# Two joined transformer blocks on one core: the norm between the blocks folded into the next stage, the second block's mixer reordered, start and tail changed

## The chip, the core and the metric

One core of a Trainium2 chip runs the whole program. Its engines are TensorE (PE, with its weight loads as PEld), VectorE (DVE), ScalarE (ACT), GpSimd (POOL) and SyncE (SP), which only issues transfers here. The metric is the time of one execution on the device in microseconds, the median of several runs. SBUF is the on-chip memory with 128 partitions, PSUM the eight banks into which TensorE writes.

## What is computed

Two different blocks follow each other on x with 256 tokens and 1024 channels in fp32. Each has two layers of FFN, mixer, FFN and ends in an RMS norm; the second block takes the normed output of the first.

```
for l in range(2):                                   # both blocks have this shape
    x = x + 0.5 * swiglu(rmsnorm(x, ffn1_norm[l]), ...)
    x = x + mixer(rmsnorm(x, mix_norm[l]))           # block 1: attention, gated recurrence, memory
    x = x + 0.5 * swiglu(rmsnorm(x, ffn2_norm[l]), ...)   # block 2: RWKV-7 group and retention group
x = rmsnorm(x, final_norm)
```

The second block's mixer projects to r, k, v and the low-rank parts, makes kk = k * k_k of unit length per head, runs the recurrence S <- S diag(w) + (S a) b^T + v k^T in chunks of 64 tokens, and beside it a retention group with rotary positions; both are gated and go through w_out.

## The kernel before

**Weights.** Every weight matrix comes in units of 1 MB (128 x 2048 fp32) through a ring of three slots in `raw`. `split_hi` (line 301, ScalarE) rounds a unit to `w_hi`, `split_lo` (line 306, VectorE) writes the remainder to `w_lo`, and TensorE multiplies high by high and low, and low by high (`mm3`, line 321; `mm`, line 326, also for all products that are not split). The next load into a slot waits for `lo_ready`, the next split for `unit_used`. Each engine has its own program in a fixed order; semaphores join them (`need` waits for a named step of another engine).

**Stages.** A stage number n counts FFNs and mixers. An FFN (`ffn_pe`, `ffn_act`, `ffn_dve`, from line 401) runs over 11 tiles: two hidden units and one output unit each. Its input is x times the norm's gain, split into `x_hi` (line 348, ScalarE) and `x_lo` (line 357, VectorE) by the stage in front of it, so that its first products need no statistics. `square_act` (line 352), `sq_sum_dve` (line 366) and `norm_pe` give the sum of squares in PSUM; `norm_dve` (lines 377 and 381) scales it and takes the reciprocal of the root that `norm_act` (line 373) takes, and the hidden values are multiplied by `rms` afterwards.

**Between the blocks** stands a stage of its own (`mid_stage`, function `between`): norm of x, x scaled by gain and rms on VectorE (line 2479), then x_hi, x_lo, squares and their sum for the next FFN. TensorE does only `norm_pe` there. The end has the same norm, with the gain on ScalarE (line 2445) and the product with `rms` on VectorE (line 2493).

**The second mixer** (`mix2_pe`, `mix2_act`, `mix2_dve`, from line 1729) has 18 units: LORA, K, UP, R, V, RQK, RV, RG and OUT2. The length of kk comes from four products with `sum_pairs` into 8 rows, a root, a reciprocal on VectorE (line 1941) and four products with `spread` back to 128 rows. The rotation of the retention's q and k (`rqk_rot`) stands after both RV units, and three VectorE steps follow (lines 1969 to 1971) before the scores `n` and `nt` may use their PSUM banks. Then come five levels (`LEVELS2`) that invert a triangular matrix by doubling: `w1` products, ScalarE's copy of w1 (line 1811), `z` and `zl` products, VectorE's predicated copies `take` (line 1895). Between them `first_fill` and `second_fill` put other products into banks 6 and 7, each of which VectorE or ScalarE must empty before the next. Both RG units run after the levels. A loop over the chunks (c from 1 to 3) passes the state between TensorE and VectorE (`new_u` line 2021, `new_state` lines 2029 and 2030); `y_centred` and the output units follow.

**SBUF.** Temporary tiles lie in an arena of 4 KB slots from `base`; `at(name, slot, ...)` places them by hand. `keep_warm(k, bank)` (line 1373) issues k products of a zero tile.

## Time and profile before

| | us |
|---|---|
| median of 3 runs | 2482.17 |
| the runs | 2477.22 to 2484.57 |
| profiled execution | 2484.07 |
| its span, first to last instruction | 2482.3 |
| TensorE busy in it | 2423.2 |
| VectorE, ScalarE, GpSimd busy | 1796.7, 1204.1, 111.6 |
| mean granted TensorE clock | 0.988 |

### The profile page before, as it was taken

The numbers are of one execution on the slowest core, as the hardware profiler recorded it, in microseconds if no ns is written. First come the engines' busy times: TensorE is split into PE (matmuls) and PEld (weight loads), VectorE is DVE, ScalarE is ACT, GpSimd is POOL, SyncE is SP. The second block draws the span as 40 slices with busy tenths as digits, with TensorE's granted clock in tenths as the row PEclk, the third lists the DMA queues.
The fourth block names the chain that finished last, engine by engine and source line by source line (L and its number), as shares of the span: only waits on it lengthen the run. The fifth ranks groups of instructions, "written<-read, shape, count | busy, mean of one in ns | idle before, by whom it ended". The sixth has DMA issues, their size and how long they took to land.

```text
span 2482.3 us, 46884 instructions
## 1 busy us (share of the span) xinstructions
PE 2423.2 (98%) x20196; PEld 2246.5 (91%) x20196; DVE 1796.7 (72%) x1608; ACT 1204.1 (49%) x1210; POOL 111.6 (4%) x71
## 2 busy tenths in 40 slices
PE   7999999999999999999998999999999999999998
PEld 6999999999899999999997999898998999988997
DVE  7877777777787767868777777756767767756766
ACT  5445656544544456555444445634445445635443
POOL 0000251000000004400000000000000000000000
PEclk9999999999999999999998999999999999999999
DMA  8555444565555555445554555413555655503652
GB/s 272 194 187 180 138 147 127 170 203 186 170 191 195 172 164 156 136 153 171 194 191 132 193 186 164 151 37 113 193 187 168 202 186 161 170 20 119 191 187 96
DMA packets 322751, 406.68 MB, mean 164 GB/s; under 512 B 6464, under 2 KB 291136, under 8 KB 322368
## 3 DMA queue, kind: packets, MB, share of 16 engines
q1 hardware_dynamic: 321472, 400.58, 50.0%
q10 hardware_dynamic: 1152, 4.22, 0.5%
q8 instruction: 103, 1.69, 0.3%
q14 instruction: 24, 0.20, 0.0%
HBM read 403.72 MB, written 1.05 MB: 163 GB/s over the span
## 4 chain that ended last, share of the span: by engine, by line
PE 93%; DVE 4%; ACT 2%; issue 0%; DMA 0%; SPq 0%; DVEq 0%; ACTq 0%
PE ps L326 48%; PE ps L321 44%; DVE w_lo L306 1%; ACT w_hi L301 1%; ACT x_hl L348 1%; DVE sq L366 1%; DVE x_hl L357 0%; PE ps L1390 0%; PE ps L2086 0%; DMA raw<-in_w_ffn_in 0%; ACT sq L352 0%; DVE x L540 0%; DVE x L2074 0%; DVE rms L381 0%; ACT k_t L1035 0%
## 5 line engine op out<-in xcount | busy, mean ns | idle before, releaser
L306 DVE TENSOR_TENSOR w_lo<-raw,w_hi 128x2048 fp32r<-128x2048 f32 x384 | 883.3, 2301 | 260.0 <-ACT w_hi L301 252.2
L326 PE MATMUL ps<-x_hl,w_hi 128*128 128x512 f32 x2816 | 989.9, 396 | 22.1 <-DVE w_lo L306 14.8
L301 ACT CAST w_hi<-raw 128x2048 fp32r<-128x2048 f32 x384 | 731.6, 1906 | 420.1 <-PE ps L321 209.0
L326 PE MATMUL ps<-x_hl,w_lo 128*128 128x256 f32 x2816 | 782.7, 278 | 0.0
L326 PEld LDWEIGHTS ps<-x_hl,w_hi 128*128 128x128 f32 x2816 | 529.9, 188 | 145.1 <-issue 22.9
L326 PEld LDWEIGHTS ps<-x_hl,w_lo 128*128 128x128 f32 x2816 | 530.5, 188 | 0.4
L321 PE MATMUL ps<-x_hl,w_hi 128*128 128x256 f32 (+1 forms) x2176 | 398.6, 285 | 0.6 <-DVE x_hl L357 0.6
L321 PE MATMUL ps<-h_hi,w_hi 128*128 128x256 f32 x1408 | 394.7, 280 | 0.0
L321 PE MATMUL ps<-h_hi,w_lo 128*128 128x256 f32 x1408 | 393.1, 279 | 0.0
L321 PE MATMUL ps<-h_lo,w_hi 128*128 128x256 f32 x1408 | 392.9, 279 | 0.0
L321 PEld LDWEIGHTS ps<-x_hl,w_hi 128*128 128x128 f32 (+1 forms) x2176 | 340.1, 192 | 4.6 <-issue 3.5
L321 PE MATMUL ps<-x_hl,w_lo 128*128 128x256 f32 x1088 | 308.4, 283 | 0.0
L321 PEld LDWEIGHTS ps<-h_hi,w_hi 128*128 128x128 f32 x1408 | 264.2, 188 | 4.4
L321 PEld LDWEIGHTS ps<-h_hi,w_lo 128*128 128x128 f32 x1408 | 264.7, 188 | 0.0
L321 PEld LDWEIGHTS ps<-h_lo,w_hi 128*128 128x128 f32 x1408 | 263.6, 187 | 0.0
L321 PEld LDWEIGHTS ps<-x_hl,w_lo 128*128 128x128 f32 x1088 | 208.8, 192 | 0.0
L424 ACT CAST h_hi<-hid 128x512 fp32r<-128x512 f32 x88 | 54.6, 621 | 300.4 <-PE ps L321 216.4
L420 ACT ACTIVATE silu_a<-ta 128x512 f32<-128x512 f32 x88 | 55.7, 633 | 261.2 <-DVE ta L473 261.2
L465 DVE TENSOR_REDUCE ta<-ps 128x512 f32<-128x1024 f32 x88 | 107.2, 1218 | 48.1 <-PE ps L326 47.5
L490 DVE TENSOR_TENSOR h_lo<-hid,h_hi 128x512 fp32r<-128x512 f32 x88 | 60.9, 692 | 101.2 <-ACT h_hi L424 101.2
L465 DVE TENSOR_REDUCE tb<-ps 128x512 f32<-128x1024 f32 x88 | 107.2, 1218 | 0.0
L477 DVE TENSOR_TENSOR silu_a<-silu_a,rms 128x512 f32<-128x512 f32 x88 | 61.0, 693 | 55.9 <-ACT silu_a L420 55.9
(437 smaller groups left out, 2739.0 us busy)
## 6 DMA issues: line engine op xcount, KB each, us to landing
raw<-in_w_ffn_in SPq DMA_DIRECT2D x88, 1024.0 KB, 5.1
raw<-in_w_in SPq DMA_DIRECT2D x74, 1024.0 KB, 5.3
raw<-in_w_ffn_out SPq DMA_DIRECT2D x44, 1024.0 KB, 4.9
raw<-in_ffn_w_gate SPq DMA_DIRECT2D x44, 1024.0 KB, 5.3
raw<-in_ffn_w_up SPq DMA_DIRECT2D x44, 1024.0 KB, 5.3
raw<-in_ffn_w_down SPq DMA_DIRECT2D x44, 1024.0 KB, 4.8
raw<-in_w_out SPq DMA_DIRECT2D x16, 1024.0 KB, 5.0
raw<-in_w_mem_kv SPq DMA_DIRECT2D x8, 1024.0 KB, 4.9
```

The costliest lines, as they stand in the source:

```text
L301: nc.scalar.copy(w_hi[:, slot, :], raw[:, slot, :]).then_inc(hi_ready, 1)
L306: nc.vector.tensor_tensor(w_lo[:, slot, :], raw[:, slot, :], w_hi[:, slot, :].bitcast(F32), ALU.subtract).then_inc(lo_ready, 1)
L321: mm = nc.tensor.matmul(out_ap, l, r, start=first and n == 0, stop=last and n == 2, skip_group_check=True)
L326: return nc.tensor.matmul(out_ap, l, r, start=first, stop=last, skip_group_check=True)
L348: nc.scalar.activation(x_hi[:, c, :], x[:, c, :], ACT.Copy, scale=gain(c)).then_inc(xhi_ready, 1)
L366: nc.vector.tensor_tensor(sq[:, 0, :, :], sq[:, 0, :, :], sq[:, p, :, :], ALU.add).then_inc(sq_summed, 1)
L420: nc.scalar.activation(silu_a[:, :, :], ta[:, :, :], ACT.Silu).then_inc(silu_done, 1)
L424: nc.scalar.copy(h_hi[a][:, :, :], hid[:, :, :]).then_inc(hh_done, 1)
L465: nc.vector.tensor_reduce(dst[:, :, :], parts, AX, ALU.add).then_inc(signal, 1)
L477: nc.vector.tensor_tensor(silu_a[:, :, :], silu_a[:, :, :], rms2, ALU.mult).then_inc(sr_done, 1)
L490: nc.vector.tensor_tensor(h_lo[a][:, :, :], hid[:, :, :], h_hi[a][:, :, :].bitcast(F32), ALU.subtract).then_inc(hl_done, 1)
```

## The change

Seven edits, all in the order of the work or in how a norm is written; the 406 MB of weights and their products stay.

1. The first unit of the first FFN is loaded, rounded and subtracted in two halves, and TensorE waits for each half by itself. 36 zero products are issued before it.
2. The stage between the blocks is gone (`joint_stage` is the second block's first FFN). The last FFN of block one prepares x times `joint_gain` = final_norm x ffn1_norm. The statistics of both norms come from one `norm_pe`: the usual sum of squares and, with `gain_rows` (a tile that `spread_gain_dve` writes in the FFN before), the sum of squares times final_norm squared, eight more fp32 products. Logarithms and exponentials replace root and reciprocal. x itself is scaled later, by `scale_x_dve`, during the FFN.
3. kk's length: two products with `head_ones` into 128 rows, then a logarithm and an exponential on ScalarE; root, reciprocal and `spread` go.
4. The rotation stands between the two RV units; `nt` comes before `n`; the first retention scores come before the first level, and all later fills one place earlier. RG0 runs inside the last level, in bank 6.
5. ScalarE's split 14 stands behind the copy of `akv` and split 16 behind the first half of `ret_hi`; VectorE's split 13 stands inside the first level. The gating of the retention output is in halves.
6. In the chunk loop the products of s_rk with v (`y_rk`) of chunks 2 and 3, and two pieces of the first output unit, stand between the state steps.
7. Tail: 14 zero products, statistics from the sum of three pairs and the fourth pair by itself, logarithm and exponential, the gain of three pairs on GpSimd and of the fourth on ScalarE.

The arena's base moves to a multiple of 512 bytes plus 448. The diff, cut to its core and moved eight columns to the left; removed lines of the fills and of VectorE's chunk loop are in the functions printed above:

```diff
...
-base = (nc.sbuf_base + 31) // 32 * 32
+base = (nc.sbuf_base + 63) // 512 * 512 + 448
...
+def first_half_hi(act):
+    act.wait_ge(half_loaded, 16)
+    nc.scalar.copy(w_hi[:, 0, 0:UNIT // 2], raw[:, 0, 0:UNIT // 2]).then_inc(half_hi, 1)
...
+    act.wait_ge(unit_used, 1)
+    nc.scalar.copy(w_hi[:, 0, UNIT // 2:], raw[:, 0, UNIT // 2:]).then_inc(hi_ready, 1)
...
+    nc.scalar.preload_act_table_set("natural_log_exp_and_others")
+    act.wait_ge(stats_done, n + 1)
+    nc.scalar.activation(joint[0][:, :], ps[:, 3, 0:T], ACT.Ln, scale=1.0 / D,
+                         bias=eps_cols[:, 0:1]).then_inc(joint_log1, 1)
+    act.wait_ge(joint_log1, 1)
+    nc.scalar.activation(joint[1][:, :], joint[0][:, :], ACT.Exp, scale=-1.0).then_inc(sqrt_ready, 1)
+    nc.scalar.activation(block_r[:, :], joint[0][:, :], ACT.Exp, scale=-0.5).then_inc(block_r_ready, 1)
+    act.wait_ge(var_ready, n + 1)
+    nc.scalar.activation(var[:, :], var[:, :], ACT.Ln, scale=1.0 / D,
+                         bias=eps_cols[:, 0:1]).then_inc(joint_log2, 1)
+    act.wait_ge(joint_sum, 1)
+    nc.scalar.activation(rms[:, :], var[:, :], ACT.Exp, scale=-0.5).then_inc(rms_ready, 1)
...
+def scale_x_dve(dve):
+    dve.wait_ge(block_r_ready, 1)
+    for c in range(DC):
...
+    dve.wait_ge(x_scaled, DC)
...
+        pe.wait_ge(gain_spread, 1)
+        for c in range(DC):
+            pe.wait_ge(sq_ready, n * 4 + c // 2 + 1)
+            mm(ps[:, bank, T:2 * T], gain_rows[:, c, :], sq[:, c // 2, c % 2, :], c == 0, False)
+        pe.wait_ge(sq_summed, n * 3 + 3)
+        for a in range(2):
+            last = mm(ps[:, bank, 0:T], C("ones"), sq_sum[:, a, :], False, a == 1)
...
+    n = final_stage
+    keep_warm(14, 5)
+    pe.wait_ge(sq_summed, n * 3 + 2)
     for a in range(2):
-        last = mm(ps[:, bank, 0:T], C("ones"), sq[:, 0, a, :], a == 0, a == 1)
+        mm(ps[:, 6, 0:T], C("ones"), sq[:, 0, a, :], a == 0, False)
+    pe.wait_ge(sq_ready, n * 4 + 4)
+    for a in range(2):
+        last = mm(ps[:, 6, 0:T], C("ones"), sq[:, 3, a, :], False, a == 1)
     last.then_inc(stats_done, 1)
...
+    nc.scalar.activation(var[:, :], ps[:, 6, 0:T], ACT.Ln, scale=1.0 / D,
+                         bias=eps_cols[:, 0:1]).then_inc(var_ready, 1)
+    act.wait_ge(var_ready, n + 1)
+    nc.scalar.activation(rms[:, :], var[:, :], ACT.Exp, scale=-0.5).then_inc(rms_ready, 1)
...
-    cols(q, 0, w_in_a(0))
+    if q == 0:
+        halves_ = raw[:, 0, :].rearrange("p (k n) -> p k n", k=DC)
+        sp.dma_start(halves_[:, 0:DC // 2, :], w_in_a(0)[:, 0:DC // 2, :]).then_inc(half_loaded, 16)
+        ring_load(sp, q, 0, halves_[:, DC // 2:, :], w_in_a(0)[:, DC // 2:, :])
...
+    nc.scalar.preload_act_table_set("natural_log_exp_and_others")
...
-    A(nc.scalar.activation(head_stat[0:8, :], head_stat[0:8, :], ACT.Sqrt), "kk_sqrt")
-    nc.scalar.preload_act_table_set("natural_log_exp_and_others")
+    A(nc.scalar.activation(kk_sq[:, :, :], kk_sq[:, :, :], ACT.Ln), "kk_ln", True)
+    A(nc.scalar.activation(kk_sq[:, :, :], kk_sq[:, :, :], ACT.Exp, scale=-0.5), "kk_r")
...
-    need(act, tensor="v_nat")
+    need(act, tensor="v_nat", vector="kk_unit")
...
-        split(13 + h)
+        if h == 0:
+            split(13)
...
+    natural(akv, 6, "akv")
+    split(14)
     level_copy(2, 0)
     level_copy(2, 1)
-    natural(akv, 6, "akv")
...
+    natural(b_nat, 6, "b_nat")
...
-    natural(b_nat, 6, "b_nat")
+    need(act, vector="gate_bias")
+    scaled(g_t, g_t, "ln_x_w", "gate_gain")
...
+    split(15)
+    ret_silu(0)
+    ret_silu(1)
     nc.scalar.preload_act_table_set("natural_log_exp_and_others")
-    need(act, vector="ret_out")
-    A(nc.scalar.copy(ret_hi[:, :, :], o_ret[:, :, :]), "ret_hi")
+    ret_high(0)
+    split(16)
+    ret_high(1)
...
-    V(TS(head_stat[0:8, :], ps[0:8, 6, 0:T], 1e-24, None, ALU.max), "kk_var")
+    V(TS(kk_sq[:, :, :], bank2(6), 1e-24, None, ALU.max), "kk_var")
...
-    need(dve, scalar="kk_sqrt")
-    V(nc.vector.reciprocal(head_stat[0:8, :], head_stat[0:8, :]), "kk_r")
...
-    need(dve, tensor="kk_spread")
-    times(kk, bank2(6), "kk_unit")
+    need(dve, scalar="kk_r")
+    times(kk, kk_sq[:, :, :], "kk_unit")
...
         take(z_up, 0, hp, 2 + hp, ("z_up", -1, hp))
...
         if i == 0:
-            ret_scores(0)
+            ret_scores(1)
         elif i == 1:
-            masked(s_ak, "strict_up64", "ak")
-        elif i == 3:
+            need(dve, tensor="o_ret")
+            V(nc.vector.tensor_copy(o_ret[:, :, :], bank2(6)), "o_ret")
+        elif i == 2:
             masked(s_rk, "incl_up64", "rk")
+        elif i == 4:
+            used(U_RG)
...
                 need(dve, tensor=("zl", i, hp))
...
-            need(dve, tensor="o_ret")
-            V(nc.vector.tensor_copy(o_ret[:, :, :], bank2(6)), "o_ret")
+            masked(s_ak, "strict_up64", "ak")
+            split(13)
+        elif i == 2:
+            for c in range(4):
+                V(STT(out=bonus[:, c, :], in0=bonus[:, c, :], scalar=col("ln_x_b", c), in1=g_t[:, c, :],
+                      op0=ALU.add, op1=ALU.mult), ("gate_bias", c) if c < 3 else "gate_bias")
+        elif i == 3:
+            need(dve, scalar="o_ret_r")
+            times(o_ret, o_ret_sq[:, :, :], "o_ret_normed")
     masked(s_rb, "incl_up64", "rb")
...
     split(15)
+    used(U_RG + 1)
+    V(TTo(ret_g[:, 2:4, :], pair(1), rms_n(2), ALU.mult), ("ret_g", 1))
...
+    def ret_out(b):
+        need(dve, scalar=("ret_g", b), vector="o_ret_normed")
...
+    def ret_low(b):
...
+    ret_out(0)
     new_u(1)
     new_state(1)
...
+    ret_low(0)
     new_u(2)
     new_state(2)
...
+    ret_out(1)
     new_u(3)
...
     split(16)
     for b in range(2):
...
-    for f in range(4):
-        last = mm(ps[0:8, 6, 0:T], C("sum_pairs")[:, 8 * f:8 * f + 8], kk_sq[:, f, :], f == 0, f == 3)
+    for b in range(2):
+        last = mm(ps[:, 6 + b, :], C("head_ones"), kk_sq[:, 2 * b:2 * b + 2, :])
...
-    need(pe, vector="kk_r")
...
-    tensor_sig(last, "kk_spread")
...
-    need(pe, vector="kk_unit")
+    need(pe, vector="kk_var")
...
+        if h == 0:
+            need(pe, vector="rqk")
+            for b in range(2):
+                last = mm(ps[:, b, :], C("rot_ret"), rqk[:, 2 * b:2 * b + 2, :])
+            tensor_sig(last, "rqk_rot")
+    need(pe, vector=["bonus", "a_hat", "b_hat"])
+    scores(rate, sig_w, 2, "nt")
+    need(pe, vector="rqk_turned")
     scores(sig_w, rate, 0, "n")
-    need(pe, vector="bonus")
-    scores(rate, sig_w, 2, "nt")
...
         tensor_sig(last, ("ret_s", a))
...
+            need(pe, scalar="akv", vector="r_hat")
+            scores(kh_t, r_t, 6, "rk")
+        elif i == 3:
+            need(pe, scalar="o_ret_ln")
+            naturals(sig_w, 6, "a_nat")
+        else:
+            need(pe, scalar="b_nat")
+            w_in(U_RG, 6)
...
+    def second_fill(i):
+        if i == 0:
+            need(pe, vector=[("ret_s", 1), "k_hat"])
+            scores(kh_t, sig_w, 6, "ak")
...
+            need(pe, vector="o_ret", scalar="v_nat")
+            for tt in range(TT):
+                last = on_tokens(s_ak, v_nat, 6 + tt, tt)
+            tensor_sig(last, "akv")
+        elif i == 2:
+            need(pe, scalar="o_ret_sq", vector="rk")
...
+            need(pe, scalar="a_nat")
...
             naturals(kh_t, 0, "k_nat")
...
+            need(pe, vector=("ret_g", 0))
...
+    need(pe, scalar=("ret_v", 1, 1))
+    ret_scores(0)
...
-    for c in range(NCH):
-        last = intra(c, v_nat, s_rk, c < 2)
-    tensor_sig(last, ("y", "rk"))
+    for c in range(2):
+        tensor_sig(intra(c, v_nat, s_rk, True), ("y_rk", c))
     need(pe, scalar=[("w_t", 0), ("w_t", 1)])
-    w_in(U_RG, 0)
...
-        need(pe, tensor=("y", "rk") if c == 1 else ("y", c - 2))
+        need(pe, tensor=("y_rk", c))
...
+            need(pe, vector=("ret_lo", 0))
+            output(0, [4])
         if c == 1:
...
+            tensor_sig(intra(c + 1, v_nat, s_rk), ("y_rk", c + 1))
+    output(0, [5])
...
+    need(pe, vector=("ret_lo", 1))
+    output(0, [6, 7])
     for b in range(2):
         need(pe, scalar=("y_sq", b))
...
+    for p in range(DC // 2 - 1):
+        x_there(pool, final_stage, p)
+        gains = vec[:, o + 2 * p:o + 2 * p + 2].unsqueeze(2).broadcast_to([P, 2, T])
+        nc.gpsimd.tensor_tensor(xn[:, 2 * p:2 * p + 2, :], x[:, 2 * p:2 * p + 2, :], gains,
+                                ALU.mult).then_inc(pairs_scaled, 1)
...
-    split_hi(act, 0, 0)
+    first_half_hi(act)
+    second_half_hi(act)
...
+    for c in (6, 7):
+        ins_ = nc.scalar.activation(xn[:, c, :], x[:, c, :], ACT.Copy, scale=col("final_norm", c))
+    ins_.then_inc(last_scaled, 1)
+    final_norm_act(act)
...
+        if n == joint_stage:
+            joint_norm_dve(dve, q)
+        else:
+            norm_dve(dve, n, q, 3)
+        extra = {joint_stage - 1: {0: spread_gain_dve}, joint_stage: {0: scale_x_dve}}.get(n, {})
...
+    keep_warm(36, 0)
...
```

## Rows read from the trace of the kernel before

**Rows 1.** The page: busy time of TensorE, and the chain that ended last by engine.

```profile
PE 2423.2 (98%) x20196; PEld 2246.5 (91%) x20196; DVE 1796.7 (72%) x1608; ACT 1204.1 (49%) x1210; POOL 111.6 (4%) x71
...
PE 93%; DVE 4%; ACT 2%; issue 0%; DMA 0%; SPq 0%; DVEq 0%; ACTq 0%
```

**Rows 2.** Windows: stretch, its length, busy us by engine, granted clock, DMA share, GB/s.

```profile
1331.70:1345.30 13.60, 6.67 (x18) 5.12 (x19) 10.71 (x22) 7.71 (x15) 0.00 (x0) 0.50 0.01 5
1580.90:1584.20 3.30, 3.30 (x18) 3.30 (x17) 2.25 (x5) 3.30 (x6) 0.00 (x0) 0.50 0.67 236
1611.70:1621.80 10.10, 7.92 (x198) 7.65 (x200) 7.20 (x7) 2.17 (x4) 0.00 (x0) 0.50 0.33 105
1686.70:1693.50 6.80, 5.58 (x25) 3.36 (x26) 5.04 (x6) 2.41 (x4) 0.00 (x0) 0.50 0.01 4
```

**Rows 3.** Tail in order of time (start, us, engine, idle before); GpSimd's costliest group.

```profile
2471.58 1.94 PE L326 MATMUL ps<-sq,cst 128*128 128x256 f32 x4 [2.97 <-DVE sq L366]
...
2474.50 0.42 ACT L373 ACTIVATE var<-var 128x256 f32<-128x256 f32 x1
2474.95 1.75 DVE L381 RECIPROCAL rms<-var 128x256 f32<-128x256 f32 x1 [0.97 <-ACT var L373]
2476.74 2.50 DVE L2493 TENSOR_TENSOR xn<-xn,rms 128x512 f32<-128x512 f32 x4
...
L900 POOL TENSOR_TENSOR hg_kq<-hg_d,hg_q 128x512 f32<-128x512 f32 x16 | 30.1, 1881 | 1.3
```

**Rows 4.** Second mixer, first layer: the spread's group, then TensorE in order of time.

```profile
L326 PE MATMUL ps<-var,cst x16: 374/374/478, 1578.2 to 2144.2; 8*128 8x256 f32 x16
...
1607.27 1.88 PE L326 MATMUL ps<-rqk,cst 128*128 128x512 f32 x4
1612.98 1.99 PE L326 MATMUL ps<-rate,sig_w 64*64 64x64 f32 x64 [3.84 <-DVE rqk L1971]
1614.75 1.93 PE L326 MATMUL ps<-sig_w,rate 64*64 64x64 f32 x64
1617.57 3.68 PE L326 MATMUL ps<-z_up,n_low 64*64 64x64 f32 x64 [0.89 <-issue]
...
1622.35 1.15 PE L326 MATMUL ps<-w,z_low 64*64 64x64 f32 x32
...
1629.01 1.10 PE L326 MATMUL ps<-sig_w,kh_t 64*64 64x64 f32 x62
```

**Rows 5.** Its chunk loop, TensorE in order of time, waits in brackets.

```profile
1687.03 1.12 PE L326 MATMUL ps<-s_rb,u_nat 64*64 64x64 f32 x16 [0.72 <-DVE u_nat L2021]
1689.04 3.75 PE L326 MATMUL ps<-y_t,cst 128*128 128x512 f32 x4 [0.89 <-DVE y_t L2054]
```

**Rows 6.** The start, all engines, in order of time.

```profile
10.30 1.90 ACT L301 CAST w_hi<-raw 128x2048 fp32r<-128x2048 f32 x1 [0.75 <-DMA raw<-in_w_ffn_in]
...
12.23 2.29 DVE L306 TENSOR_TENSOR w_lo<-raw,w_hi 128x2048 fp32r<-128x2048 f32 x1 [2.07 <-ACT w_hi L301]
...
14.78 0.76 PE L326 MATMUL ps<-x_hl,w_hi 128*128 128x512 f32 x1 [14.78 <-DVE w_lo L306]
...
18.22 0.39 PE L326 MATMUL ps<-x_hl,w_hi 128*128 128x512 f32 x1
...
18.84 1.91 ACT L301 CAST w_hi<-raw 128x2048 fp32r<-128x2048 f32 x1 [2.76 <-issue]
...
26.96 1.16 DVE L465 TENSOR_REDUCE ta<-ps 128x512 f32<-128x1024 f32 x1
```

**Rows 7.** Windows of the block turn and an ordinary one; TensorE at an ordinary turn.

```profile
1328.68:1367.03 38.35, 28.68 (x145) 23.83 (x144) 30.44 (x39) 19.20 (x26) 0.00 (x0) 0.82 0.34 110
1905.70:1931.47 25.77, 24.88 (x140) 20.99 (x139) 23.25 (x27) 16.23 (x20) 0.00 (x0) 1.00 0.49 162
...
678.94 1.13 PE L326 MATMUL ps<-sq,cst 128*128 128x256 f32 x4 [0.58 <-DVE sq L366]
679.91 0.81 PE L326 MATMUL ps<-zero_w 128*128 128x512 bf16 x3
```

209 lines of the change are left out of this document (106 added, 103 removed).

## The prediction, made before the changed kernel was run

> **What bounds the kernel now.** I read the page first, then the windows of the low-clock stretches, then the order of time around every place where TensorE stood still. TensorE is busy 98% of the span and carries 93% of the chain that ended last [rows 1]. So a microsecond leaves the program only if it is a wait of TensorE, a stretch in which TensorE ran at its lower clock, or matmul work that disappears. What VectorE, ScalarE and the transfers gain counts only where TensorE waits for them.
>
> The places are few: the start (14.78 us before the first matmul), the turn between the two blocks, two spots in each of the two second mixers, and the tail. Each has a cost beside the wait itself: a granted clock of 0.50, the 1.2 GHz level [rows 2]. What came before each fall is in the same trace: 2.97 us of nothing at the tail [rows 3], 3.84 us of nothing in the mixer [rows 4], waits of up to 0.9 us in a row in the chunk loop [rows 5]. The second mixer of the second layer repeats the last two (falls at 2174.8 and 2249.9 with the same lengths). Everything between, the eight FFN stages and the first mixers, is untouched, and I let it stand.
>
> **The start.** ScalarE turns idle 0.75 us before 10.30, so at 9.55, and then waits for the whole first unit; its copy takes 1.90 us, VectorE's subtraction 2.29 us, and TensorE begins at 14.78 [rows 6]. With the unit in halves, copy and subtraction of the first half take half of that each: 9.55 + 0.95 + 1.2 + 0.1 = 11.8, if the first half has landed by 9.55. I estimate that it has (the whole was there at 10.30 and half of it is 512 KB); if it is as late as the whole, it is 12.6. The first matmuls run slow, one of 512 columns in 0.76 us where a later one takes 0.39 [rows 6]; that lasts about 2.7 us, so 1.3 us is lost. The 36 zero matmuls are meant to have the clock up before. They begin at about 1 us; one of the same shape costs (0.81 - 0.39) / 2 = 0.21 us at the high clock [rows 7], 0.43 at the low one. If the clock rises after as long as it did before, they end near 10; if it never rises, 15.4 us after they began, at 16.4, the start is 1.6 us later than now. I take the first. But the gain of 4.2 us is not all kept: the third unit's copy starts at 18.84, at the end of 2.76 us in which ScalarE had nothing to do, which I read as the data. Behind it stand the copy 1.9, the subtraction 2.3, the reciprocal 1.75 [rows 3] and the reduction 1.16 that frees the PSUM bank [rows 6]: 18.84 + 7.1 = 26.0. Before, the reduction ended at 28.12 and TensorE took the bank some 0.7 us later, at 28.8 by my count of its matmuls. So TensorE will now wait there, and the start brings 28.8 - 26.0 = **2.8 us** (bounds 1.4 and 4.2).
>
> **Between the blocks.** Before, from the last output matmul of block one to the first output matmul of the next FFN are 38.35 us; the ordinary turn from a layer to the next, with the same work, takes 25.77 [rows 7]. The fold makes this turn an ordinary one, because x times the joined gain is there without any norm. It adds eight fp32 matmuls of 128x256, two passes each. Passes of that form cost (1.13 - 0.38) / 3 = 0.25 us; 16 of them are 3.4 to 4.0 us, I take 3.7. They need only the squares and so also fill the 0.58 us wait for the summed squares [rows 7]. 38.35 - 25.77 - 3.7 + 0.5 = **9.4 us** (9.0 to 10.0). The longer chain behind the statistics (a logarithm and two exponentials on ScalarE, two 128x256 operations on VectorE, then the reduction: some 3.6 us) runs under the second hidden unit, 5.5 us of TensorE, and misses the 1.75 us reciprocal. The eight multiplications that scale x (0.4 us each, 3.2 in all) and the copy that spreads the gain stand on VectorE behind the first low part; VectorE is idle more than a quarter of an FFN (its 23.25 busy us of 25.77 in the turn are the worst case, [rows 7]) and TensorE has some 6 us until it needs the next sum. Cost nothing; if that cover were gone, 3.2 us.
>
> **Second mixer, kk norm.** The sum over pairs and the new head sum are the same eight half-passes' worth of TensorE. The spread of the reciprocal (8 passes of 256 columns from 8 rows, 0.374 us each with overlap [rows 4], start to start 0.24) goes: 1.9 us per layer, **3.8 us**. In the first layer the clock was at 0.50 for 3.3 us just behind it, with TensorE busy all of it [rows 2]; in the second it was not. I give these 3.3 / 2 = **1.7 us** to the change, because the 8-row passes are the only unusual thing in front of them; below, 0. VectorE loses a reciprocal and gains a wider maximum; ScalarE gains two 128x1024 activations for one of 8x256, by my estimate under one split's time (1.9 us, [rows 6]). Units are 5.7 us of TensorE apart there and no wait over 0.1 us is seen in that stretch before, so this costs nothing; with the cover gone, 1.9 per layer.
>
> **Second mixer, from the rotation to the first level.** Between the start of the rotation at 1607.27 (1.88 us of work) and the first z product at 1622.35 are 15.1 us [rows 4]: a wait of 3.84 us for VectorE's three steps on rqk, the two score sets at 1.99 and 1.93 us, a wait of 0.89, and the w1 products at 3.68 us, all at the low clock from 1611.7 [rows 2]. With the rotation in front of the second RV unit, the three steps lie under 5.75 us of matmuls. At the high clock the work is 1.7 (rotation) + 2 x 0.95 (a score set is 62 passes in 1.10 us less its tail, [rows 4]) + 0.9 (the first retention scores, which now stand there and cover the copies of n) + 1.9 (w1, half of 3.68) = 6.4. So 8.7 us less. New waits I count by queue: the second retention scores wait for VectorE's product, which stands behind the four predicated copies (0.4 us); the third level waits for ScalarE's w1 copy, which now stands behind split 14, 1.9 us of work begun when akv is copied (0.4 us); 0.2 for what I can't see. 7.7 us per layer, **15.4 us** (bounds 10 and 17.5). All other fills keep an engine's whole turn between a product and its use. The unit RG0 moves into the last level, where its split is long done; it is work moved, not work removed.
>
> **Second mixer, chunk loop.** TensorE waits 0.72 and 0.89 us [rows 5] and, with the three shorter waits ahead of them, 2.8 in all. The products y_rk of chunks 2 and 3 (0.5 us each) and two output pieces (0.65 us each) move into these holes. Against it: VectorE now has the gate product and ret_out in front of new_u(1), 1.4 us; TensorE has 1.7 us of its own there. And RG1 alone (5.75 us, before 11.5) covers splits 14 and 15; they end some 1.3 us before it does. I leave 0.8 us of new waits: 2.0 us per layer, **4.0 us** (0 to 5.6). The low clock from 1686.7 to 1693.5, in which TensorE was busy 5.58 us [rows 2] with, above all, the 3.75 us centring [rows 5], goes if the holes cause it: 2.4 per layer, **4.8 us** (0 to 5.6).
>
> **The tail.** TensorE stops at 2468.61, the statistics run 2471.58 to 2473.52 at the low clock, and the final products begin at 2476.74 [rows 3]. After: 14 zero matmuls of 0.21 us fill 3.0 us; four fp32 matmuls at the high clock take 1.8 instead of two at the low one's 1.94: statistics at 2473.4, as now. Then two activations of 0.42 and their hops instead of scaling, table load, root and 1.75 us reciprocal: products from 2474.4, **2.4 us** earlier (1.5 to 3). GpSimd must have three products of 128x512 by then, at 1.5 to 1.95 us each (1.88 for the costliest line, [rows 3]) from about 2466.5: done at 2472.3, a cover of 2 us. The Trainium skill speaks against this: by "GPSIMD Engine Reference", Specifications, the engine shares its SBUF interfaces with VectorE and contends with instructions that read two SBUF inputs. The two sums of squares are such instructions; even if each grew by a whole 0.69 us the statistics would be ready some 0.6 us later, and no run shows it yet.
>
> The moved arena base changes addresses only, and no row of this trace shows that an address matters; I count zero.
>
> **Sum.** 2.8 + 9.4 + 3.8 + 1.7 + 15.4 + 4.0 + 4.8 + 2.4 = 44.3 us. The profiled execution took 2484.07 us, 1.8 over its span of 2482.3; from it the sum gives 2439.8. The median of the runs is 2482.17, 1.9 lower: **2438 us**.
>
> **Rivals.** (a) The clock still falls. The waits go, but the narrow 64-row products and short holes go on taking the clock down, after the scores and in the chunk loop, as [rows 2] show in both layers. For it: in the chunk loop the waits before the fall were under 0.8 us each. Against it: from 1622 to 1686 the same products ran without a wait over 0.6 us at the high clock. Then 4.8 us of the loop are not won and half of the 7.9 busy us at 1611.7 [rows 2] per layer, another 7.9: 2438 + 12.7 = 2451. The Trainium skill has this as a rule: "TensorE: Matmul & The Clock Gate", "A second HAM failure mode: psum-queue depth-cycling", says that small idle times between groups of matmuls alone can make the clock go down and up. (b) The queues bite: in-order VectorE and ScalarE hold split 14 or 15 in front of something TensorE needs at once. One VectorE split of 2.3 and one ScalarE split of 1.9 exposed per layer, and 0.7 for ret_out: 9.8 us, 2448. For it: five new waits on one chain of PSUM banks 6 and 7; against it: the spacings counted above. (c) Slower: the levels, now with a wide unit inside and waits at other places, run at the low clock throughout. A score set then takes 1.93 instead of 1.10 us; some 41 us of such products per layer at +0.75 are 62 us in both: 2438 + 62 = 2500. It decides from 59 us of low-clock products on; no level stretch in this trace does so, hence little chance. (d) The change doesn't do what it says: the turn between the blocks stays long because another operand of the next hidden unit is late, 2447; the ordinary turns speak against it.
>
> **How the numbers follow.** Forecast 0.60, (a) 0.16, (b) 0.16, (d) 0.05, (c) 0.03. The range reaches from 2431 (start and loop at their good ends, no new waits) to 2452 (rival a). A measurement of this kernel tells about 0.3%, 7.4 us, from no change; cases of 0.96 lie below 2474.7, 0.01 within, 0.03 above.
>
> **What would show it.** First matmul on real data at 11.8; the turn at 29 us; no wait over 1 us and a granted clock of 1.00 from the rotation to the centring; x products of the tail 2.4 us nearer to the last matmul. A third unit that starts at 24.5 would refute the data limit at the start; clock falls without waits would refute the cause that I give them.

## The result and the profile of the changed kernel

| | before | changed |
|---|---|---|
| median, us | 2482.27 (6 runs, 2477.22 to 2484.57) | 2440.68 (6 runs, 2440.07 to 2441.24) |
| span of the profiled execution, us | 2482.3 | 2439.0 |
| TensorE busy | 2423.2 us | 2417.3 us |
| waits of TensorE over 0.15 us, summed over the trace | 50.1 us | 14.1 us |
| stretches of low clock ahead of the tail | 6 | none |

The ratio is 0.9835 (95% interval 0.9822 to 0.9847). The forecast was 2438 us with a range of 2431 to 2452: the time lies 2.7 us above the forecast and inside the range. By the medians the change brings 41.6 us. By the two profiled executions it brings 43.3 us, because the one of the kernel before was 1.8 us above its median and the one of the changed kernel lies at its median; the parts below are read from the profiles.

The page of the changed kernel, TensorE's busy time and the chain that ended last:

```profile
PE 2417.3 (99%) x20238; PEld 2238.2 (92%) x20238; DVE 1787.9 (73%) x1606; ACT 1200.7 (49%) x1207; POOL 114.7 (5%) x74
...
PE 93%; DVE 4%; ACT 2%; issue 1%; DMA 0%; SPq 0%; DVEq 0%; ACTq 0%
```

The span fell by 43.3 us and the waits by 36.0. Busy time fell by only 5.9 us, but the zero matmuls make up 23.4 us of it where they made up 9.6: the rest of TensorE's work took 19.7 us less, most of it matmuls that ran at the low clock before. Windows of the turn between the blocks (as the first of [rows 7]) and of the second mixer of the first layer from the second RV unit to the output products (stretch, length, busy us of PE, PEld, DVE, ACT, POOL, clock, DMA share, GB/s):

```profile
1326.47:1354.84 28.37, 28.06 (x155) 23.94 (x154) 22.07 (x32) 17.96 (x24) 0.00 (x0) 1.00 0.45 149
1583.00:1700.00 117.00, 114.32 (x2216) 104.91 (x2216) 76.18 (x91) 52.31 (x68) 0.00 (x0) 1.00 0.25 81
```

38.35 us have become 28.37, at a granted clock of 1.00 (2.4 GHz) where the mean was 0.82. In the mixer 2.7 us of waits are left in 117. The places of [rows 4] and [rows 5] in order of time (start, us, engine, line, tiles, wait in brackets):

```profile
1585.58 1.88 PE L344 MATMUL ps<-rqk,cst 128*128 128x512 f32 x4
1593.12 1.16 PE L344 MATMUL ps<-sig_w,rate 64*64 64x64 f32 x64
1594.11 1.11 PE L344 MATMUL ps<-rate,sig_w 64*64 64x64 f32 x64
1595.15 0.94 PE L344 MATMUL ps<-rqk 64*128 64x128 f32 x12
1596.02 2.08 PE L344 MATMUL ps<-z_up,n_low 64*64 64x64 f32 x64
1598.13 0.94 PE L344 MATMUL ps<-rqk 64*128 64x128 f32 x12
1599.00 1.15 PE L344 MATMUL ps<-w,z_low 64*64 64x64 f32 x32
...
1617.71 0.97 PE L344 MATMUL ps<-w,z_low 64*64 64x64 f32 x26 [0.60 <-ACT w L1923]
...
1664.76 1.96 PE L344 MATMUL ps<-y_t,cst 128*128 128x512 f32 x4
```

The waits of 3.84 and 0.89 us are gone; the score sets take 1.16 and 1.11 us where they took 1.99 and 1.93, the centring 1.96 where it took 3.75. The one wait over 0.3 us that is left there is the 0.60 in front of the third level: w1's copy stands behind split 14.

The start, ScalarE and TensorE; compare [rows 6]:

```profile
9.23 1.03 ACT L310 CAST w_hi<-raw 128x1024 fp32r<-128x1024 f32 x1
10.48 1.05 ACT L320 CAST w_hi<-raw 128x1024 fp32r<-128x1024 f32 x1 [0.22 <-DMA raw<-in_w_ffn_in]
...
11.62 0.47 PE L344 MATMUL ps<-x_hl,w_hi 128*128 128x512 f32 x1
...
19.04 1.91 ACT L298 CAST w_hi<-raw 128x2048 fp32r<-128x2048 f32 x1 [3.62 <-issue]
...
26.16 0.49 PE L344 MATMUL ps<-x_hl,w_hi 128*128 128x512 f32 x1 [1.47 <-DVE ta L567]
```

The first product on real data is at 11.62 instead of 14.78, but the third unit's copy is where it was (19.04, before 18.84), and TensorE waits 1.47 us in front of the third unit. The tail, all engines; compare [rows 3]:

```profile
2426.16 1.04 POOL L2545 TENSOR_TENSOR xn<-x,vec 128x512 f32<-128x512 f32 x1 [0.37 <-DVE x L642]
...
2426.48 0.28 PE L339 MATMUL ps<-h_hi,w_lo 128*128 128x256 f32 x1
...
2426.60 3.20 PE L344 MATMUL ps<-zero_w 128*128 128x512 bf16 x14
...
2427.41 1.48 DVE L401 TENSOR_TENSOR sq<-sq 128x512 f32<-128x512 f32 x2
...
2429.63 1.89 PE L344 MATMUL ps<-sq,cst 128*128 128x256 f32 x8
...
2432.51 2.50 DVE L2625 TENSOR_TENSOR xn<-xn,rms 128x512 f32<-128x512 f32 x4 [3.63 <-ACT rms L484]
```

The last FFN matmul of TensorE, the first of these PE lines, stood in the kernel before at

```profile
2468.33 0.28 PE L321 MATMUL ps<-h_hi,w_lo 128*128 128x256 f32 x1
```

From its start to the four products were 8.4 us, now 6.0: they come 2.4 us nearer. But from the start of the products to the end are 6.5 us where they were 5.5.

### Where the time came from

The same event is found in both traces, and the difference of its two times is noted; what it grows by over a stretch is the gain of that stretch. Each part comes from one execution of each kernel. Stretches in which nothing was edited moved by up to 0.8 us in such a comparison, and by about 2 us where an FFN stage ran slow (last section), so smaller differences between parts say nothing.

| stretch | forecast, us | measured, us |
|---|---|---|
| start | 2.8 | 2.7 |
| first block behind the start (not changed) | 0 | -0.5 |
| turn between the blocks | 9.4 | 10.0 |
| second mixer, first layer | 15.7 | 15.9 |
| second mixer, second layer | 14.0 | 13.5 |
| FFN stages of the second block (not changed) | 0 | 0.3 |
| tail | 2.4 | 1.4 |
| sum | 44.3 | 43.3 |

### The profile page after: what moved, and what is told of

It reads as the page before. It is cut to its first block, busy times and chain, and to the rows that moved or that the text cites. A ratio compares the mean times of both kernels' runs of the same rounds, so it can differ in the third digit from the quotient of the medians.

```text
span 2439.0 us, 46973 instructions
## 1 busy us (share of the span) xinstructions
PE 2417.3 (99%) x20238; PEld 2238.2 (92%) x20238; DVE 1787.9 (73%) x1606; ACT 1200.7 (49%) x1207; POOL 114.7 (5%) x74
## 4 chain that ended last, share of the span: by engine, by line
PE 93%; DVE 4%; ACT 2%; issue 1%; DMA 0%; SPq 0%; DVEq 0%; ACTq 0%
PE ps L344 47%; PE ps L339 45%; DVE w_lo L303 1%; ACT w_hi L298 1%; ACT x_hl L366 1%; DVE sq L401 0%; DVE x_hl L391 0%; DMA raw<-in_w_ffn_in 0%; PE ps L1501 0%; PE ps L2217 0%; ACT sq L370 0%; DVE x L2205 0%; DVE x L642 0%; ACT k_t L1146 0%; DVE m_lo L1268 0%
```

## The experiments

All but one are edits of the changed kernel, so their medians stand against its 2440.7 us. They ran in later batches; the kernel before had medians of 2482.5 to 2483.3 us in these, against 2482.3 in the first, so differences of medians under 1 us aren't read. Parts are read from the profiled execution as growth over a stretch, as above.

### Does idle time bring the clock down, or do narrow products?

The rotation is put back behind both RV units, first alone, then with zero matmuls in the wait.

```
             for h in range(2):
                 project_rows(pe, q, U_RV + h, ...)
-                if h == 0:
-                    need(pe, vector="rqk")
-                    rotation
-            need(pe, vector=["bonus", "a_hat", "b_hat"])
+            need(pe, vector="rqk")
+            rotation
+            # second kernel only: need(pe, scalar="v_nat"); keep_warm(16, 4)
+            need(pe, vector=["rqk_turned", "bonus", "a_hat", "b_hat"])
             scores(rate, sig_w, 2, "nt")
-            need(pe, vector="rqk_turned")
             scores(sig_w, rate, 0, "n")
```

> The rotation stands behind both RV units again. My theory, wait and clock: TensorE waits 3.8 us per layer, the clock falls to 0.50 behind that wait, and the score sets, the first retention scores and w1 take 4.5 us more: 8.3 per layer, 2457 us. Rival, the wait alone: 3.8 per layer with the clock at 1.00, 2448.3 us.

> As the run before, with 16 zero matmuls (3.4 us) in the wait. If idle time brings the clock down, it stays at 1.00 and the run is 3.8 us per layer over the changed kernel: 2448.3 us. Rival, the narrow 64-row products bring it down by themselves once the unit in front of them ends: the clock falls all the same behind the scores, 2457 us.

Measured: 2452.2 us (2450.1 to 2454.6) without and 2450.5 us (2450.0 to 2453.4) with the zero matmuls. TensorE in order of time and the window of the low clock without the zero matmuls, then TensorE in order of time with them:

```profile
1598.09 1.16 PE L344 MATMUL ps<-sig_w,rate 64*64 64x64 f32 x64 [3.84 <-DVE rqk L2091]
1599.07 1.89 PE L344 MATMUL ps<-rate,sig_w 64*64 64x64 f32 x64
1600.90 1.65 PE L344 MATMUL ps<-rqk 64*128 64x128 f32 x12
```

```profile
1599.20:1602.50 3.30, 3.30 (x82) 2.96 (x74) 2.20 (x4) 1.07 (x2) 0.00 (x0) 0.50 0.02 5
```

```profile
1594.37 3.62 PE L344 MATMUL ps<-zero_w 128*128 128x512 bf16 x16
1598.37 1.16 PE L344 MATMUL ps<-sig_w,rate 64*64 64x64 f32 x64 [0.38 <-DVE rqk L2091]
1599.35 1.11 PE L344 MATMUL ps<-rate,sig_w 64*64 64x64 f32 x64
1600.39 0.94 PE L344 MATMUL ps<-rqk 64*128 64x128 f32 x12
```

The same 64x64 products behind the same delay run at 1.89 us a set after an idle wait and at 1.11 after a filled one, in both layers. So idle time is the cause here, and narrow products alone don't bring the clock down. The delay costs 3.9 us per layer in the filled kernel; idle, it costs 5.4 and 4.9, so the clock's part is 1.0 to 1.5 us per layer and not the 4.5 that I expected (the medians alone, 1.8 us apart with overlapping runs, wouldn't tell it): the stretch was 3.4 us long, where the kernel before had one of over 10 us [rows 2]. The next run asks why.

### What makes the low stretch long

The first of the two kernels above (no zero matmuls), with the first retention scores moved in front of the score sets:

```
             need(pe, vector=["rqk_turned", "bonus", "a_hat", "b_hat"])
+            need(pe, scalar=("ret_v", 1, 1))
+            ret_scores(0)
             scores(rate, sig_w, 2, "nt")
             scores(sig_w, rate, 0, "n")
...
-            need(pe, scalar=("ret_v", 1, 1))
-            ret_scores(0)
             for i in range(len(LEVELS2)):
```

> As the third run (rotation behind both units), and the first retention scores stand in front of the two score sets, so that nothing covers the copies of n: a second wait of some 0.9 us follows 4 us behind the long one, as in the kernel before. If a second hole prolongs the low clock, the stretch is 6.8 to 10.2 us long instead of 3.4, and the run takes 8 us per layer more than the changed kernel: 2457 us. Rival, the length of the stretch has nothing to do with the second hole: 3.4 us of low clock, 6.2 per layer, 2453 us.

Measured: 2457.2 us (2454.6 to 2457.6). TensorE in order of time in the first layer, and the windows of the low clock in both layers:

```profile
1596.92 1.65 PE L344 MATMUL ps<-rqk 64*128 64x128 f32 x12 [3.83 <-DVE rqk L2091]
1598.50 1.98 PE L344 MATMUL ps<-sig_w,rate 64*64 64x64 f32 x64
1600.26 1.93 PE L344 MATMUL ps<-rate,sig_w 64*64 64x64 f32 x64
1602.98 1.23 PE L344 MATMUL ps<-z_up,n_low 64*64 64x64 f32 x35 [0.80 <-ACT n_low L1919]
```

```profile
1595.90:1602.70 6.80, 5.27 (x140) 4.86 (x140) 3.43 (x4) 0.45 (x1) 0.00 (x0) 0.50 0.01 2
2155.70:2159.00 3.30, 3.30 (x128) 3.19 (x120) 1.34 (x2) 0.00 (x0) 0.00 (x0) 0.50 0.02 5
```

The median is the one expected of the second hole. But the trace doesn't carry the mechanism: the first layer's stretch is twice as long as the second's, though the code is the same, and it begins 2.8 us after TensorE stopped and so takes in part of the wait; the layers cost 7.5 and 5.4 us. In the two profiles of code that has both old waits (before, and the run on the turn below) this place shows stretches of 10.2, 10.2, 10.2 and 3.4 us. That a wait near 4 us brings the clock down is shown, eight times of eight; what sets the length of the stretch stays open.

### The chunk loop: short holes

TensorE's order in the loop as before (all y_rk first, no output pieces inside), then the same with three zero matmuls in front of each wait:

```
-            for c in range(2):
-                tensor_sig(intra(c, v_nat, s_rk, True), ("y_rk", c))
+            for c in range(NCH):
+                tensor_sig(intra(c, v_nat, s_rk, c < 2), ("y_rk", c))
...
-                if c == NCH - 1:
-                    need(pe, vector=("ret_lo", 0))
-                    output(0, [4])
...
-                if c < NCH - 1:
-                    tensor_sig(intra(c + 1, v_nat, s_rk), ("y_rk", c + 1))
-            output(0, [5])
...
+                # second kernel only, ahead of the waits for ("state", c) and ("u", c)
+                keep_warm(3, 0)
```

> TensorE's order in the chunk loop as before: all four y_rk products ahead of the loop, no output pieces in it; VectorE's and ScalarE's order stay new. My theory: the waits in the loop are 2.8 us per layer instead of 0.9, and the clock falls to 0.50 at the centring and costs 2.4 more: 4.3 per layer, 2449.3 us. Rival: holes under 0.9 us don't bring the clock down, 1.9 per layer, 2444.5 us.

> As the run before, with three zero matmuls (0.64 us) ahead of each of the six waits in the loop. If idle time brings the clock down, it stays at 1.00 to the centring; the zero matmuls take 3.8 us per layer where 2.8 were waits, so 2.9 per layer over the changed kernel: 2446.5 us. Rival, the narrow 64-row products do it by themselves: low clock at the centring all the same, 2451 us.

Measured: 2447.3 us (2446.0 to 2451.5; the profiled execution is the slowest of the four) with the holes idle, 2450.4 us (2449.5 to 2450.6) with them filled. In the first of them the two layers went different ways. The centring of both, and the windows behind the last short wait:

```profile
1667.70 3.75 PE L344 MATMUL ps<-y_t,cst 128*128 128x512 f32 x4 [0.88 <-DVE y_t L2186]
...
2221.15 1.96 PE L344 MATMUL ps<-y_t,cst 128*128 128x512 f32 x4 [0.89 <-DVE y_t L2186]
```

```profile
1665.90:1672.60 6.70, 5.82 (x27) 3.60 (x26) 4.70 (x5) 1.78 (x3) 0.00 (x0) 0.50 0.13 32
2219.50:2226.20 6.70, 5.74 (x46) 4.43 (x47) 4.81 (x6) 1.78 (x3) 0.00 (x0) 1.00 0.13 40
```

The same waits (0.52, 0.51, 0.40, 0.88), the same products, and the clock falls once and not the other time: 4.9 us and 1.6 us. Over the kernels with these holes idle it fell five times of six, with them filled, but for the last one of 0.88 us, never (two layers), with the new order never (20 layers of ten profiles). So the holes do it, but not each time: the same code gave both outcomes. The filled kernel has no low clock and is slower all the same, 4 us above what I expected: 3.9 us per layer in the profile where I had 2.9, since the zero matmuls are time spent on the path, and one FFN stage of that execution ran 1.9 us slower besides (below). Its median alone, 2450.4 us, would have spoken for the rival; the clock in the trace speaks against it. Filling with real work is what pays.

### kk norm

The old norm is put back: the sum over pairs, root and reciprocal on 8 rows, and the spread.

```
-            for b in range(2):
-                last = mm(ps[:, 6 + b, :], C("head_ones"), kk_sq[:, 2 * b:2 * b + 2, :])
+            for f in range(4):
+                last = mm(ps[0:8, 6, 0:T], C("sum_pairs")[:, 8 * f:8 * f + 8], kk_sq[:, f, :], f == 0, f == 3)
...
+            need(pe, vector="kk_r")
+            for f in range(4):
+                last = mm(ps[:, 6 + f // 2, ...], C("spread")[0:8, f * P:(f + 1) * P], var[0:8, :], ...)
```

> The old normalisation of kk: sum over pairs into 8 rows, root, reciprocal, and the spread from 8 rows. My theory: the spread costs TensorE 1.9 us per layer, and the passes from 8 rows bring a stretch of low clock behind them in the first layer's second mixer, 1.7 us: 2440.7 + 3.8 + 1.7 = 2446.2 us. Rival: the 8-row passes have nothing to do with the clock, it stays at 1.00 and 2444.5 us come out. Second rival: the new norm was hidden work for work and nothing changes, 2440.7.

Measured: 2447.6 us (2446.1 to 2449.1); 2.9 us in the first layer's mixer, 3.3 in the second's. The spread and the window behind it, second layer:

```profile
2117.32 1.99 PE L344 MATMUL ps<-var,cst 8*128 8x256 f32 x8
...
2119.60:2122.90 3.30, 3.30 (x18) 3.30 (x17) 2.72 (x5) 3.30 (x8) 0.00 (x0) 0.50 0.75 264
```

This time the low clock is behind the second layer's spread and not behind the first's [rows 2]. In six layers that have the spread (before, this run, the run on the turn) it came twice, each time right behind those passes and with TensorE busy throughout; in 22 layers of the eleven profiles without it, never. So the passes from 8 rows are the likely cause, in some executions only. The layer without a low clock costs about 1 us more than the spread itself; of it 0.5 us is at the place of the norm, and I didn't follow the rest. The layer with it costs only 0.4 us more than the other, where half of 3.3 us would be 1.7; a wait of 0.60 us at the first state products, which the changed kernel has in that layer, is gone in it. So the price of this stretch is not shown to be 1.7 us.

### The two ends: zero matmuls, and the data at the start

The changed kernel without `keep_warm(36, 0)` at the start and without `keep_warm(14, 5)` at the tail:

> Both runs of zero matmuls are out: the 36 at the start and the 14 at the tail. Start: if the third unit is limited by its data, as I hold, the first two units run slower by some 1.3 us at the low clock, the 1.47 us wait in front of the third unit swallows it, and the third unit starts at 26.2 as in the changed kernel; if TensorE's own work sets that place, it starts at 27.5. Tail: the four fp32 matmuls start some 0.7 us earlier, right behind the sum; if 2.3 us of nothing are enough to bring the clock to 0.50, they take 3.8 us instead of 1.89 and the products begin 1.2 us later against the last FFN matmul; if 2.3 us are too short for that, they begin 0.7 us earlier.

Measured: 2442.4 us (2441.8 to 2443.6). At the start the first product takes 0.77 us instead of 0.47 and the first two units 1.9 us longer; the third unit starts at 26.6. All data of this execution were 0.46 us later (third unit's copy at 19.50), so the wait of 1.47 us did swallow what the cold clock cost: as long as the third unit waits for its data, the 36 zero matmuls bring nothing. The tail, in order of time:

```profile
2428.95 1.48 DVE L401 TENSOR_TENSOR sq<-sq 128x512 f32<-128x512 f32 x2
...
2430.48 1.99 PE L344 MATMUL ps<-sq,cst 128*128 128x256 f32 x8 [2.18 <-DVE sq L401]
...
2433.47 2.50 DVE L2624 TENSOR_TENSOR xn<-xn,rms 128x512 f32<-128x512 f32 x4 [3.04 <-ACT rms L483]
```

After 2.18 us of nothing the four matmuls take 1.99 us, the time of the high clock, where after 2.97 us they took 1.94 for half as many passes [rows 3]. The products begin 5.4 us behind the start of the last FFN matmul, against 6.0 with the zero matmuls: these end 0.7 us after the sum of squares that they bridge, and so hold up the statistics. At the tail they cost 0.6 us. The median is 1.7 us higher all the same. In the profile 0.45 us of it is the late data, and 0.8 and 0.2 us came up in the two second mixers, where nothing was edited; the rest isn't explained.

Then the transfer of mem, moved behind the first split of the loop:

```
             second_half_hi(act)
-            act.dma_start(memn[:, :, :], ins["mem"]).then_inc(mem_loaded, 16)
...
             def rest_loads(act):
+                act.dma_start(memn[:, :, :], ins["mem"]).then_inc(mem_loaded, 16)
```

> The transfer of mem (1 MB) is issued behind the first split of the loop instead of in the middle of the start. If the third unit is limited by its data, its copy starts some 2.8 us earlier than 19.04 (1 MB at the 350 to 386 GB/s that the queues move there), the wait of 1.47 us in front of the third unit goes, and everything behind is 1.4 us earlier: 2439.3 us. If ScalarE's or VectorE's own order sets the third unit, the copy stays within 0.3 us of 19.04 and nothing moves: 2440.7.

Measured: 2439.5 us (2439.1 to 2441.1). The third unit's copy on ScalarE:

```profile
16.50 1.91 ACT L298 CAST w_hi<-raw 128x2048 fp32r<-128x2048 f32 x1 [1.14 <-issue]
```

It starts 2.5 us sooner, the wait of 1.47 us is gone, and from the third unit on every event is 1.4 us earlier. The data limit is shown: what the halves won in front of the third unit was capped by a transfer that nobody needs yet.

### The turn between the blocks: how much of it was the clock

The kernel before, with 12 zero matmuls ahead of the statistics between the blocks and 28 behind them:

```
-            run(pe, ffn, mix1_pe, mix2_pe, lambda: norm_pe(pe, mid_stage))
+            def between():
+                for _ in range(12): mm(ps[:, 7, :], zero_w[:, :], zeros)
+                norm_pe(pe, mid_stage)
+                for _ in range(28): mm(ps[:, 7, :], zero_w[:, :], zeros)
+            run(pe, ffn, mix1_pe, mix2_pe, between)
```

> The kernel before with zero matmuls in both waits between the blocks, 12 ahead of the statistics and 28 behind them. If the waits cause the low clock of 13.7 us there, it is gone and its share of the turn with it: TensorE was busy 6.7 us of it, so 3.3 us: 2479 us, and 6.1 of the 9.4 us of the turn are left to the order of the work. Rival, the fall has another cause or the filling delays what it stands in front of: no gain, 2482.3 us.

Measured: 2478.1 us (2475.4 to 2481.9) against 2482.5 (2479.1 to 2484.7) of the kernel before in the same runs, ratio 0.9986 (0.9977 to 0.9996). The place itself:

```profile
1331.78:1345.40 13.62, 12.59 (x63) 8.25 (x64) 11.09 (x22) 7.87 (x15) 0.00 (x0) 1.00 0.03 9
```

The clock stays at 1.00 and the stretch to the next layer stage is 3.1 us shorter. So 3.1 of the turn's 10.0 us were the clock, and by subtraction 6.9 are the order of the work, that is, the fold. (The profile as a whole is 8.7 us shorter: in its second mixers three of the four low stretches behind the waits are shorter and the one behind the spread is missing, at places that the edit doesn't touch.)

### The arena's base and the two splits

```
-        base = (nc.sbuf_base + 63) // 512 * 512 + 448
+        base = (nc.sbuf_base + 31) // 32 * 32
...
-                if h == 0:
-                    split(13)
+                split(13 + h)             # ScalarE: split 14 ahead of the copies of n
...
-            split(14)                     # its new place, behind akv's copy
...
+            split(13)                     # VectorE: ahead of the predicated copies
...
-                    split(13)             # its new place, behind s_ak
```

> Two small parts undone, told apart by their places: the arena's base is aligned to 32 bytes as before, and in the second mixers ScalarE's split 14 stands in front of the copies of n and VectorE's split 13 in front of the predicated copies, as before. Base: I expect no stage outside the second mixers to change by over 0.3 us; if addresses matter, all stages with VectorE or ScalarE on their path do. Splits: the copies of n come 1.9 us later and w1 of the first level waits some 1.5 us, while the 0.60 us wait of the third level goes: 0.9 per layer, 2442.5 us. Rival: there is slack for both splits and the place doesn't matter, 2439.5.

Measured: 2450.4 us (2448.1 to 2451.8), 8 us above what I expected. The second mixers hold a small part of it: waits of 0.86 and 0.54 us in front of n's users, none at the third level, 0.8 and 0.6 us per mixer, 1.4 in all. The rest is elsewhere, where the code is the same. Against the changed kernel the same events are later by 1.4 us at 369, 2.2 at 672, 3.6 at 1028 and 4.9 at 1522: a slow, even growth. The products that read tiles of the arena have changed their length; one such tile in the changed kernel and then in this one:

```profile
L339 PE MATMUL ps<-c_hi,w_lo x80: 275/277/282, 312.4 to 1012.9; 128*96 128x256 f32 x48, 128*128 128x256 f32 x32
```

```profile
L339 PE MATMUL ps<-c_hi,w_lo x80: 274/281/286, 313.2 to 1016.5; 128*96 128x256 f32 x48, 128*128 128x256 f32 x32
```

(The three numbers are the shortest, the median and the longest in ns.) By the program, the arena begins at byte 148416 of a partition in the kernel before, 148928 in the changed one and 148480 here: 448, 448 and 0 modulo 512. So the change's new formula keeps the residue that the old one had by luck, and the 64 bytes of the joined gain would otherwise have cost some 8 us by the medians (5.8 in the profile).

The traces say more. From start to start the products that stream h_hi and h_lo (both in the arena) are 117.8 to 118.1 ns apart on average in each of the thirteen other profiles, and 118.9 here; those with c_hi and c_lo 123.1 there and 125.6 here, those with om_hi and om_lo 121.1 and 124.0. Where TensorE streams x_hl, which lies outside the arena, in products of 128x512, every second product starts after 349.2 ns, within the 348.6 to 350.1 of the others. Summed over all groups of equal neighbours these distances grow by 6.9 us, and the last FFN ends 8.2 us later, of which the splits are 1.4. So the address acts through TensorE's products. Which property of it counts isn't shown: the three bases also differ modulo 128 (64, 64 and 0), and only one pair was tried.

### A combined version

The changed kernel with mem's transfer late; ScalarE's split 14 behind the gain of the gate; and at the tail no zero matmuls, only one addition of squares on VectorE, placed ahead of its last update of x, three pairs of sums through TensorE, and all four products on GpSimd:

```
             natural(akv, 6, "akv")
-            split(14)
...
             scaled(g_t, g_t, "ln_x_w", "gate_gain")
+            split(14)
...
-            keep_warm(14, 5)
-            pe.wait_ge(sq_summed, n * 3 + 2)
+            pe.wait_ge(sq_summed, n * 3 + 1)
             for a in range(2): mm(ps[:, 6, 0:T], C("ones"), sq[:, 0, a, :], a == 0, False)
-            pe.wait_ge(sq_ready, n * 4 + 4)
-            for a in range(2): last = mm(ps[:, 6, 0:T], C("ones"), sq[:, 3, a, :], False, a == 1)
+            for p in (2, 3):
+                pe.wait_ge(sq_ready, n * 4 + p + 1)
+                for a in range(2): last = mm(ps[:, 6, 0:T], C("ones"), sq[:, p, a, :], False, p == 3 and a == 1)
...
-            for p in range(DC // 2 - 1):  # GpSimd's products
+            for p in range(DC // 2):
```

> The changed kernel with what the runs point to. The transfer of mem is late (1.4 us). ScalarE's split 14 stands behind the gain of the gate, so that the third level's w1 products don't wait (0.6 per layer, 1.2). The tail has no zero matmuls: VectorE adds only the first two pairs of squares, in front of its last update of x, the other two pairs go through TensorE, and GpSimd makes all four products (1.04 us each); the statistics end some 1.7 us sooner and ScalarE is free for the logarithm: 1.6 us. Sum 4.2: 2436.5 us. Rival: the update of x on VectorE or the fourth product on GpSimd holds the tail, and 0.7 us of it are won: 2437.4.

> The changed kernel once more, beside the combined one on the same chip, to have their difference and the spread from execution to execution: 2440.7 us, all executions within 2 us of each other if what spread the kernel before (7 us) was the length of its low-clock stretches.

Measured on one chip: 2436.7 us (2435.9 to 2437.4) and, for the changed kernel again, 2441.0 us (2440.2 to 2444.8). Against the kernel before the ratio of the combined version is 0.9818 (0.9802 to 0.9835). Its tail:

```profile
2424.14 2.46 POOL L2548 TENSOR_TENSOR xn<-x,vec 128x512 f32<-128x512 f32 x2 [0.37 <-DVE x L644]
...
2424.72 2.86 PE L344 MATMUL ps<-sq,cst 128*128 128x256 f32 x12
...
2428.57 2.50 DVE L2622 TENSOR_TENSOR xn<-xn,rms 128x512 f32<-128x512 f32 x4 [3.09 <-ACT rms L484]
```

TensorE goes on without a hole, the products start 4.1 us behind the start of the last FFN matmul (6.0 in the changed kernel), and the wait at the third level is gone. The two GpSimd products take 1.42 and 1.04 us; the first of them ran beside VectorE's sum of squares (2423.98 to 2424.66), which kept its 0.68 us. The medians differ by the 4.3 us that I expected, but the profile's parts are others: 2.3 us ahead of the second block's mixers where I had 1.4, 1.7 in the two mixers for 1.2, 2.9 at the tail for 1.6, and 1.9 lost in a last FFN that ran slow. The end came 5.5 us behind the start of the products here and 6.5 in the changed kernel. In the changed kernel a transfer of instructions falls into that time. The DMA queues of its last 6.5 us (packets, MB, share of the 16 engines):

```profile
q1 hardware_dynamic: 288, 0.52, 22.4%
...
q14 instruction: 1, 0.01, 0.4%
```

In nine of the fourteen profiles queue 14 carries that packet between the start of the products and the end, and there the end comes 6.3 to 6.6 us behind them; in the five others (before, the run on the turn, kk, base and splits, combined) it doesn't, and the end comes after 5.4 to 5.6. The packet stands 4.5 to 4.9 us behind the start of the products in the nine, and the last output packets end 0.4 to 0.8 us later than in the five; in the kernel before and the run on the turn it came 0.6 and 0.3 us ahead of the products. The two go together without exception. That the packet is the cause, and that it depends on where the program's last instructions lie, is likely, but no edit was made for it alone.

## Why the prediction was right, step by step

- **Sum and median.** The sum of the parts was 44.3 us and is 43.3, so 1.0 of the 2.7 us of error is here, and in it errors of up to 1.0 us, of either sign, partly cancel. The other 1.7 us come from the last step, which took off the 1.9 us between the profiled execution and the median of the kernel before. That distance did not carry over: the executions of the changed kernel lie within 1.2 us of each other.
- **Start.** Predicted 11.8 for the first matmul, a third unit at 26.0 and 2.8 us; measured 11.62, 26.16 and 2.7. The cap by the data was the step on which the term rested, and moving mem's transfer shows it. The zero matmuls ended at 11.56 and not near 10, just ahead of the data. The prediction counts the start among the places with a granted clock of 0.50; the profile gives 1.00 there, and the slow clock shows only in the length of the products (0.76 us, then 0.39).
- **Turn.** 28.4 us where I had 29; 10.0 for 9.4 us. The fp32 matmuls of the joined statistics took 3.62 us, in the range of 3.4 to 4.0. Everything that I had costed at nothing on VectorE (the eight scalings, the spread gain) stayed at nothing: from 1328 to 1517 us TensorE has no wait over 0.1 us.
- **kk norm.** The spread was rightly 1.9 us. The 1.7 us of low clock that I gave to it read the first layer's trace, but as a property of the kernel it is a chance of two in six layers, 0.6 us each by that price, and the run that put the spread back showed no more than 0.4 to 1.0 us for it. The term isn't shown to be right, and the sum can't tell it apart.
- **Rotation to levels.** The mechanism was right: the wait, the clock behind it, and the small new waits. I had three of these, 0.4 for the second retention scores, 0.4 behind split 14 and 0.2 unseen; measured are none, 0.60 and, in the second layer, another 0.60 at the first state products. The split of the gain was not tested as I wrote it: in the kernel before the long stretch made the clock's share about 4 us per layer, but the same wait can come with a 3.4 us stretch and cost only 1.0 to 1.5. The three undone edits (rotation, chunk loop, kk) give back 13.2 of the first mixer's 15.9 us and 9.8 of the second's 13.5.
- **Chunk loop.** Waits of 0.9 us are left per layer, 0.8 were forecast. Undoing TensorE's order costs 6.6 us by the medians, where the terms were 4.0 and 4.8, 8.8 together; the clock term is the one with chance in it (4.9 us in one layer, 1.6 in the other).
- **Tail.** This term was mis-sized: 2.4 forecast, 1.4 measured. The way to the products was right in its steps: the statistics ended 5.0 us behind the start of the last FFN matmul (5.1 by the forecast), the products began 1.0 us later, and they came 2.4 us nearer. GpSimd's products take 1.04 us, not 1.5 to 1.95 (no row of before shows that form there), which only widened its cover. Without the 14 zero matmuls the products would have come 0.6 us sooner still. The step that fails is that nothing behind the products changes; the end came 0.9 us later, with a transfer of instructions between.
- **Base.** "No row of this trace shows that an address matters; I count zero" gave the right number for a wrong reason. An address does matter, by some 8 us; it didn't here because the residue stayed the same.
- **Rivals.** (a) is refuted in its form "narrow products take the clock down": filled waits keep it up in all four layers tried. Its other half, small holes, came true in five of six layers with the old order of the loop and in none with the new. The Trainium skill ("TensorE: Matmul & The Clock Gate", A second HAM failure mode: psum-queue depth-cycling) describes such small idle times between groups; the trace of the old chunk loop agrees, with holes of 0.40 to 0.88 us, and that of the new one, with holes of 0.17 to 0.27 us, does not. (b) came to 0.6 to 1.2 us per layer of the 4.9 I had priced. (c) and (d) didn't occur. The contention on SBUF interfaces that the Trainium skill names ("GPSIMD Engine Reference", Specifications) was not put to the test by the changed kernel: the two sums of squares, which read two SBUF operands, start only when GpSimd's last product has ended (2427.2 and 2427.41). VectorE's updates of x beside the products kept their 0.69 us, but they read one operand from PSUM. The combined version's trace agrees with the Trainium skill here, and the cost falls on GpSimd: beside a sum of squares its product took 1.42 us instead of 1.04, and the sum kept its length.

## What to carry to other kernels

Count idle time of TensorE twice, once as a wait and once as a risk for the clock, and fill it with work that has to be done anyway: zero matmuls keep the clock but cost what they last where they stand on the path. When a start or a tail is shortened, look for the transfer that now sets it; here one that nobody needed for many microseconds held the third unit. After any edit that adds a tensor to SBUF, compare the addresses of the tiles before and after (here 448 against 0 modulo 512) before blaming the edit.
